# Sample tokens' layer 1 on tile B's weight chunks, an earlier sample path and new unit tables in a two-layer decoder step

## The reference

```
z = gelu(h @ w_in + b_in); u = z[:, :1536]; v = rms_norm(z[:, 1536:], g_v)     # layer 1, 1024 x 3072 weights
s = causal(w_s) . v + b_s;  y += gate * ((u * s) @ w_out)                      # 1536 x 1024
q = h @ w_q                                                                    # PEER, 1024 x 2048
idx, g = top 16 of 128 x 128 product keys, for each token and each of 8 heads
out = sum over 8 heads and 16 experts of g * gelu(u_tab[idx] . h) * v_tab[idx] # rows of 1024 floats
```

## Time and profile before

| what | value |
|---|---|
| median of three runs | 2014.44 us |
| span of the profiled execution | 2136.8 us |
| that execution against the median | 1.061 |
| TensorE, VectorE, ScalarE, GpSimd busy | 72%, 62%, 17%, 55% |
| granted TensorE clock, mean | 0.814 of full |
| moved by the DMA engines | 751.57 MB, mean 352 GB/s |
| of it by GpSimd's queue, by SyncE's queue | 564.20 MB, 185.72 MB |

### The profile page before, as it was taken

How to read it: one execution, slowest core, us unless ns; L and a number is a source line. 1 busy time by engine, 2 the same in 40 slices (tenths; PEclk the granted TensorE clock), 3 DMA queues, 4 the chain that set the end, 5 groups by cost and what they waited for, 6 DMA issues and landing times.

```text
span 2136.8 us, 25746 instructions
## 1 busy us (share of the span) xinstructions
PE 1549.0 (72%) x9280; PEld 752.4 (35%) x9280; DVE 1321.9 (62%) x3189; ACT 353.4 (17%) x934; POOL 1185.7 (55%) x1097
## 2 busy tenths in 40 slices
PE   5863767867579799878785999897877741563765
PEld 2453233522135346524442456534423310111211
DVE  2369886887776555488676756587885336434442
ACT  0210121111122111112131211131312110010011
POOL 0023665566776645467646645577675257744655
PEclk8887878987687897988887897997988785777777
DMA  9868989999999999999969799999998989999998
GB/s 371 314 236 346 365 330 347 391 396 382 347 346 348 359 404 373 361 414 347 382 212 345 271 375 401 378 345 349 367 337 303 352 309 343 402 417 370 377 349 306
DMA packets 213941, 751.57 MB, mean 352 GB/s; under 512 B 27236, under 2 KB 35628, under 8 KB 213816
## 3 DMA queue, kind: packets, MB, share of 16 engines
q0 software_dynamic: 155136, 564.20, 69.8%
q1 hardware_dynamic: 58680, 185.72, 22.4%
HBM read 747.74 MB, written 2.10 MB: 351 GB/s over the span
## 4 chain that ended last, share of the span: by engine, by line
PE 43%; DVE 14%; DMA 13%; issue 12%; POOL 8%; another core or an unknown queue 7%; ACT 2%; SPq 1%; DVEq 0%; POOLq 0%; ACTq 0%
PE yacc L1274 13%; DMA vring<-in_peer_v,expert 6%; POOL uring L813 4%; PE pp L1062 4%; DVE uring L2046 4%; POOL vring L813 3%; PE pp L1036 3%; PE pp L1125 3%; PE pq L1125 2%; PE ps L1160 2%; PE ps L870 2%; PE pp L1197 1%; DMA uring<-in_peer_u,expert 1%; PE ps L1184 1%
## 5 line engine op out<-in xcount | busy, mean ns | idle before, releaser
L813 POOL DMA_INDIRECT uring<-in_peer_u,expert x512 | 571.5, 1116 | 471.1 <-DVE dots L2046 191.1
L1274 PE MATMUL yacc<-vring,diag 64*64 64x512 f32 x4096 | 659.3, 727 | 230.1 <-DMA vring<-in_peer_v,expert 118.0
L813 POOL DMA_INDIRECT vring<-in_peer_v,expert x512 | 542.2, 1059 | 430.6 <-PE yacc L1274 263.3
L2046 DVE CUSTOM_DVE_ANT_0 uring<-uring,h 128x1024 f32<-128x1024 f32 x512 | 614.9, 1226 | 201.2 <-DMA uring<-in_peer_u,expert 175.7
L1274 PEld LDWEIGHTS yacc<-vring,diag 64*64 64x64 f32 x4096 | 158.0, 154 | 589.1 <-issue 345.5
L1566 ACT ACTIVATE diag<-cst,wts 128x64 f32<-128x64 f32 (+1 forms) x528 | 155.4, 338 | 470.4 <-PE yacc L1274 229.9
L1062 PE MATMUL pp<-hT,wring 128*128 128x128 f32 x1024 | 128.9, 287 | 10.4 <-DMA wring<-in_peer_w_q 4.6
L1062 PEld LDWEIGHTS pp<-hT,wring 128*128 128x128 f32 x1024 | 124.1, 202 | 28.1 <-issue 26.2
L1929 DVE TENSOR_REDUCE arena<-arena 128x16 f32<-128x1024 f32 x64 | 77.8, 1216 | 63.8 <-ACT arena L1505 58.8
L1317 ACT ACTIVATE arena<-ps 128x512 f32<-128x512 f32 (+6 forms) x77 | 39.9, 532 | 253.4 <-remote 76.9
L1125 PE MATMUL pp<-w_uk,arena 128*128 128x512 f32 x128 | 75.3, 677 | 3.4 <-issue 2.7
(11 more groups left out here) (306 smaller groups left out, 1823.0 us busy)
## 6 DMA issues: line engine op xcount, KB each, us to landing
wring<-in_peer_w_q SPq DMA_DIRECT2D x48, 1024.0 KB
wring<-in_sg_w_in SPq DMA_DIRECT2D x48, 768.0 KB
wring<-in_w_mod SPq DMA_DIRECT2D x35, 1024.0 KB
wring<-in_sg_w_out SPq DMA_DIRECT2D x18, 1024.0 KB
uring<-in_w_mod SPq DMA_DIRECT2D x9, 1024.0 KB, 12.7
wring<-in_mla_w_o SPq DMA_DIRECT2D x9, 1024.0 KB
uring<-in_peer_u,expert POOLq DMA_INDIRECT x512
vring<-in_peer_v,expert POOLq DMA_INDIRECT x512
```

The lines of the kernel that those rows point to most:

```text
L813: pool.indirect_dma_start(ring[:, slot % RING, :], None, table[n // 3], bass.IndirectOffsetOnAxis(ap=idx, axis=0)).then_inc(land[slot % RI ...
L1274: last = pe.matmul(yacc[64 * q:64 * q + 64, r], diag[at, slot % RING, :], v[at, 512 * q:512 * q + 512], start=first, stop=final)
L2046: dve.tensor_tensor_reduce(u, u, rows_h[:, :], 1.0, 0.0, ALU.mult, ALU.add, dots[:, p % 2, i:i + 1]).then_inc(u_used, 1)
```

## The change

- S's layer 1 input product is computed in B's `sgu_v` and `sgu_u`, with the same weight chunk in the ring; its output product in B's `sgu_out`; its layer 1 query in B's layer 1 `query` stages. The 16 `sgu_s` stages, S's own `sgu_out` and the weight part of `query_s` 5 are gone. `sgu_s_mix` stands ahead of B's `sgu_mix`.
- For that, S must be through layer 0 before B's layer 1. Caches 0 to 3 come before `peer_out` 0, caches 4 to 7 between the routes of A's layer 1, and S's experts of layer 0 after four of A's eight heads. `peer_out` 3 moves to the end.
- S's buffers su_s, sv_s, sp_s, vp_s, gT_s and the gain move into `kv` and `kr`. TensorE no longer waits for the store of new_v_s.
- The five tables are new; they hold no N.

```diff
+S_AFTER = (4, 8)
-    return a0 + b0 + a1 + b1[:2] + [(2, None)] + b1[2:8] + [(5, None)] + b1[8:]
+    return a0 + b0 + a1[:S_AFTER[0]] + [(2, None)] + a1[S_AFTER[0]:] + b1[:S_AFTER[1]] + [(5, None)] + b1[S_AFTER[1]:]
-CACHES = (2, 3, 3)
+CACHES = (4, 4)
-    era1 = ([("peer_out", 0), ("sgu_init",)] + sgu(A) +
-            heads(3, (4, 4))[:1] + mods(1, 20, 24) + woven(heads(3, (4, 4))[1:], caches[CACHE0[1]:CACHE0[2]]))
-    era2 = [("peer_out", 1)] + sgu(B) + woven(heads(4, (4, 4)), caches[CACHE0[2]:])
-    era3 = [("cache_out",), ("proj", S), ("norm", S, 0, 1), ("query_s", 2), ("topk_s", 2), ("peer_out", 3)]
-    era4 = [("peer_out", 2), ("norm", S, 1, 0)] + [("sgu_s", j) for j in range(16)]
-    era4 += [("sgu_s_mix",), ("sgu_out", S), ("norm", S, 1, 1), ("query_s", 5), ("topk_s", 5)]
-    return start + era0 + era1 + era2 + era3 + era4 + [("peer_out", 4), ("peer_out", 5)]
+    era1 = ([("peer_out", 0), ("sgu_init",), ("norm", A, 1, 0)] + sgu(A) + [("norm", A, 1, 1)] +
+            heads(3, (4, 4))[:1] + mods(1, 20, 24) + woven(heads(3, (4, 4))[1:], caches[CACHE0[1]:]))
+    era2 = [("cache_out",), ("proj", S), ("norm", S, 0, 1), ("query_s", 2), ("topk_s", 2)]
+    era3 = [("peer_out", 1), ("peer_out", 2), ("norm", S, 1, 0), ("norm", B, 1, 0)] + sgu(B)
+    era3 += [("norm", S, 1, 1), ("norm", B, 1, 1)] + heads(4, (4, 4)) + [("query_s", 5), ("topk_s", 5)]
+    return start + era0 + era1 + era2 + era3 + [("peer_out", 3), ("peer_out", 4), ("peer_out", 5)]
 PLAN_PE
-1113:VV 1114:VV 1115:VVVV 1116:VVVVVVVV
+1032:VVVVVVVVVVVVVVVVVVVVVVVVVVV 1033:VVVVV
+1039:VVVVVVVVVVVVVVVVVVVVVVVVVVVVVVVVVVVVVVVVVVVVVVVVVVVVVVVVVVVVVVVVVVVVVVVVVVVVVVVVVVVVVVVVVVVVVVVVVV 1042:VVVVVV
...
 PLAN_POOL = """
...
+UUUVUUUUUUUUUUVUVVVUVVVVVVVVVUVUVUVUUUUUUUUUUUVUVVVVVVVVVVVVVVVUUUUUUUUUUUUUUUVUVVVVVVVVUVVVVVVVUUUUUUUUUUUUUUVUVVVVV
+VVVVVVUVVVVUUUUUUUUUUUUUUVUVVVVVVVVVVVUVVVVUUUUUUUUUUUUUUVUVVVVVVVVVVVUVVVVUUUUUUUUUUUUUUVUVVVVVVVVVVVUVVVVUUUUUUUUUU
+UUVVVVVVVVVVVVVVVVV
...
+                if tile == B:
+                    last = sgu_sample(w, c, 0)
+            def sgu_sample(w, c, at):
+                last = quad_matmuls(pq[:, 1], hTs[:, c, :], w[:, 0, :], SGQ, c == 0, False)
+                if c == KD - 1:
+                    last = quad_matmuls(pq[:, 1], ones[at:at + 1, 0:32], rows[at:at + 1, :], SGQ, False, True)
+                            if lhs_s is not None:
+                                last = quad_matmuls(pq[:, 0], lhs_s[:, 32 * g:32 * g + 32], w[:, c, :], QUAD,
+                                                    g == 0, g == 2 * n - 1)
+                        if n == 4:
+                            last = quad_matmuls(pq[:, 0], hTs[:, kk, :], w[:, c, :], QUAD, kk == 0, kk == KD - 1)
-                for i in range(8):
+                for i in range(8 * (n == 2)):
-                pe.wait_ge(v_out, 80)
+                if tile == B:
+                    residual(k, S, pq[:, 0:1, :], "xs")
```

More of the change, by code:

```diff
@@ L119 @@
[L119 to L123, removed]
@@ L224 @@
 MOD_ROW = 4
-CACHES = (2, 3, 3)
-CACHE0 = [sum(CACHES[:i]) for i in range(4)]
+CACHES = (4, 4)
+CACHE0 = [sum(CACHES[:i]) for i in range(3)]
 def rope_before(b):
@@ L256, in schedule, with sgu @@
                                             ("norm", A, 0, 1)] + first[:2])
-    sgu = lambda t: ([("norm", t, 1, 0)] + [("sgu_v", t, c) for c in range(KD)] + [("sgu_vnorm", t)] +
-                     [("sgu_u", t, c) for c in range(KD)] + [("sgu_mix", t), ("sgu_out", t), ("norm", t, 1, 1)])
+    def sgu(t):
+        tail = [("sgu_s_mix",)] if t == B else []
+        return ([("sgu_v", t, c) for c in range(KD)] + [("sgu_vnorm", t)] + [("sgu_u", t, c) for c in range(KD)] + tail +
+                [("sgu_mix", t), ("sgu_out", t)])
     caches = [("cache", b) for b in range(NT)]
@@ L362, in labels @@
     if kind == "sgu_out":
-        return ["row"] * (tile != S) + [f"w{i}" for i in range(6)], ["x"], ["row"] * (tile != S)
+        return ["row"] + [f"w{i}" for i in range(6)], ["x"] + ["xs"] * (tile == B), ["row"]
     if kind == "peer_out":
@@ L374, in chunk_labels @@
     return {"mla_in": ["z", "z", "qk"], "proj": ["w0", "w1", "w2", "w3"], "query": [f"w{i}" for i in range(step[-1])],
-            "query_s": [f"w{i}" for i in range(8)], "sgu_v": ["v"], "sgu_u": ["u"], "sgu_s": ["z"],
+            "query_s": [f"w{i}" for i in range(8)], "sgu_v": ["v"], "sgu_u": ["u"],
             "sgu_out": [f"w{i}" for i in range(6)]}[step[0]]
@@ L578, in begin @@
             else:
-                if not (kind in ("sgu_v", "sgu_u", "sgu_s") and SCHEDULE[j][0] == kind):
+                if not (kind in ("sgu_v", "sgu_u") and SCHEDULE[j][0] == kind):
                     j += 1
@@ L739, in _ @@
                     sp.dma_start(su, bcast(t["sg_g_v"], P)).then_inc(gv_in, 16)
+                    for q in range(4 * (tile == B)):
+                        sp.dma_start(gv_s[32 * q:32 * q + NT, :], bcast(t["sg_g_v"][:, SGQ * q:SGQ * q + SGQ], NT))\
+                          .then_inc(gvs_in, 16)
                 spot()
@@ L1470, in query_s @@
                 after(act, PE, k, "s")
+                after(act, DVE, max(j for j in range(k) if SCHEDULE[j][0] == "route"), "top")
                 signal(copy(sc[0:64, 0, :, :], ps[1][0:64, 0:256].rearrange("p (i t) -> p i t", i=2)), "s")
@@ L1526, in sgu_v @@
                         last = copy(sv[:, 512 * q:512 * q + 512], (ps[0], ps[1], pq[:, 0])[q][:, :])
+                    if tile == B:
+                        last = copy(sv_s, pq[:, 1, 0:SGQ])
                     signal(last, "v")
@@ L1587, in _ @@
                           cache=cache, sgu_v=sgu_v, sgu_vnorm=sgu_vnorm, sgu_u=sgu_u, sgu_mix=sgu_vnorm,
-                          sgu_s=sgu_s, sgu_s_mix=sgu_s_mix, proj=projection, sgu_out=projection, peer_out=peer_out,
+                          sgu_s_mix=sgu_s_mix, proj=projection, sgu_out=projection, peer_out=peer_out,
                           tables=tables)
```

178 lines of the change are left out of this document (71 added, 107 removed), and 2 rows, old and new, of the table FLOW.

## The result

| | us, median | runs | ratio to before (95%) |
|---|---|---|---|
| kernel before | 2018.8 | 4 | 1 |
| changed kernel | 2044.9 | 4 | 1.0156 (1.0120 to 1.0192) |

The account below looks back on a forecast made before the run. It took the kernel as bound by moving its 751.57 MB, at about 85% of the best rate; terms -75 - 11 + 8 + 20 + 6 + 0 + 8 = -44 us of the 2136.8 us span gave 2093, median 1973 us, range 1900 to 2065.

Parts of the forecast that it names:

- Traffic removed, -75: Last 397 us: 27.26 MB of weight chunks fewer, at 362 GB/s, saves 75 us.
- cross-check: Whole span: 1782 us before the last stage, 271 for its 195 gathers, 12 to drain: 2065, or 2107 with losses.
- Stalls at the end, -11: End: no TensorE wait for the new_v_s store (5 us), samples' second top-16 trip covered (6): -11 (-5 to -23).
- Samples' experts of layer 0, +8 (0 to +18): Samples' top-16 and trip through memory: too few free transfers, 14 us lost less 6 for the old gap.
- B's layer 1, +20 (0 to +45): B's `peer_out` to first route's end: chain of some 225 us against 208 of transfers, 17 longer; value sums also added.
- Start +6: Start: first value sums come later, at B's first norm, most of it caught up: +6 us (0 to +17).
- caches 0: Caches 2, 3 and 5 to 7 move to other stretches, same work: 0 us (-24 to +15).
- Coarser tables, +8: GpSimd's order: 38 runs of 8 or more gathers into one ring, against 9: +8 us (-10 to +100).
- No N, 0: TensorE's table: 48 small matmuls go and nobody waits for them, no term; their effect on the clock left to a rival.
- Nothing given back: Rival, whole kernel: new order closes lulls too, traffic, end stalls and 24 us beside caches gained: 1911 us; chance 0.17.
- Clock: Rival, last 104 value sums: idle TensorE gets 1.2 GHz, sums take 1.98 us, about 35 us lost: 2006; chance 0.17.
- Runs block GpSimd: Rival, every run of 8 or more gathers: GpSimd waits on a full ring, 100 us: 2060 us; chance 0.23.

Follow-up runs that it names:

- without the trips' waits: Changed kernel with the two sample steps' gathers taking row numbers from tile B's first head, so none waits for the samples' top-16: 2033.0 us, ratio 1.0051.
- the second profile of the kernel before: The kernel before, unchanged, run and profiled once more beside the first experiments: 2012.3 us, span 2010.5 us.
- The small gathers: Both kernels with every expert's gather cut to rows of 64 floats instead of 1024: span 1926.2 us for the kernel before, 1986.8 for the changed one.
- the run with 30 fewer there: Changed kernel, end-stretch u and v gathers alternating, samples' layer-0 experts behind five steps of A's layer 1 instead of four: 2083.9 us, ratio 1.0354.
- the run with the turns: Changed kernel with u and v gathers alternating from u gather 437 on, all of the last stage: 2035.1 us, ratio 1.0074.

## Why the prediction was wrong

*What bounds the kernel: wrong, and everything else follows.* I took a DMA share of 90% and a rate of 85% of the best as a bound. With 94% of the gathers' bytes gone the kernel keeps 96% of its time. The forecast asked of each stretch how many bytes it has; it had to ask which stage chain or which issuing engine ends it.

*Traffic removed, -75: the first step that failed.* The chunks' bytes are worth 35 us, nearly all in the stretch of the samples' layer 1. By place the sum still looks near: that stretch goes altogether (-175), and the 87 gathers that it covered stand alone at the end (+107), -68 in all where I had -86 for traffic and stalls. That nearness is luck. The forecast priced neither part; it had the end stretch's length only in the cross-check.

*Where the sign turned.* The sum was -44 and the two profiled spans differ by +26: 70 us. The end and the samples' layer 1 have 18 of them, about what the runs of gathers cost. B's layer 1 has 34 (+54 for +20), the queries, routes and caches 35 (for 0), the samples' query 8 (+16 for +8). The start, A's layer 1 and the +8 for coarser tables, which has no row of its own, give 25 back. So the steps that failed most are those in which I let work moved into a stage go beside the transfers.

*The scale.* The sum was put from a span of 2136.8 on the median by 0.943. That the execution was 6% long was seen, not weighed: the rates came from it. The cross-check, 1782 us up to the last stage and 271 for it, gave 2053 before its 12 us of draining and was then scaled as well; measured are 1771 and 266. Left as it was it would have forecast no gain; and since the poor execution's rates stood in it beside the right stretches, its nearness is part luck.

*Stalls at the end, -11.* The store's 22 us stood in the stretch that went, so they are in the -175. The second trip ran covered, as forecast.

*Samples' experts of layer 0, +8 (0 to +18).* The place and the lull were right: TensorE at `peer_out`, value sums behind it, three v gathers, then the trip. The price without the trips' waits is 21 us (give or take 9), where I had 14 before taking off 6 for the old gap: within its noise of that.

*B's layer 1, +20 (0 to +45): the overlap was wrong.* The chain that I had worked out, 225 us up to the end of B's first route, came out nearly as long, in part because 9 us too much at its base met 12 too little in what came in. From the samples' `peer_out` (1394), behind which B's layer 1 begins in the changed kernel, it took 228; in the second profile of the kernel before, from B's `peer_out` (1155), 155. (From B's own `peer_out`, at 1347, it took 275, with the wait for the samples' experts in it.) The end of that route in the changed kernel:

```profile
1622.08 0.24 DVE L1844 TENSOR_SCALAR gate<-eg 128x16 f32<-128x16 f32 x1
```

But I set 208 us of transfers against it and booked little more than the 17 by which the chain was longer. The small gathers show that the transfers hold up nothing there: 168 us against 112 without their bytes. B's layer 1 alone, up to its own addition, became 168 from 114: +54. Three quarters of the products are worth 19 (I had 30 for all of them in the chain); the lull at the mixes came as forecast (160 GB/s in 1520 to 1540 us). That part of the 54 is gathers moved in (77 against 48) is not shown; the run with 30 fewer there says they cost little.

*Start +6, caches 0.* The start came 7 us earlier. For the caches: queries, routes and eight caches took 35 us more, and 52 more with the small gathers (435 + 352 + 207 against 349 + 292 + 301, cut at the same additions). So it is in the engines' own order and not in the gathers' bytes.

*Coarser tables, +8.* In the end stretch the runs cost 16 us. Ahead of it no cost of their order shows; what lumps of dots and value sums cost there is in the 35 us and was not separated.

*No N, 0: nearly right.* Their removal gained 9 us (2 to 16) in the kernel before; it was not tested in the changed one, which has none.

*The rivals.* Nothing given back: wrong, it shared the premise. Clock: wrong. TensorE was granted 0.71 in the end stretch, but a value sum took 1.25 us there (120.1 us for 768 records, 8 to a sum), not over 1.5, and the run with the turns is faster at 0.67. TensorE's group in that stretch:

```profile
L1258 PE MATMUL yacc<-vring,diag 64*64 64x512 f32 x768 | 120.1, 761 | 131.9 <-ACT diag L1551 101.0 <-DMA vring<-in_peer_v,expert 30.1
```

Runs block GpSimd: nearest in time (2060), wrong in mechanism. Its waits for rings, which answer to the last of the earlier trace rows, are 412 us, under the 454 that I gave as the mark of the forecast; but the second profile of the kernel before has 369 of them, so they did grow by 43:

```profile
POOL uring L791 <- DVE dots L2033: 212.6, 86, 11.5
POOL vring L791 <- PE yacc L1258: 199.7, 146, 18.0
```

The rate up to the last stretch was 353 GB/s (724.3 MB less 98.7, in 1771 us), over my mark of 340, and the last stretch lasted 266 us. Of the marks, the weights' bytes, both lulls and this rate came out as forecast, and the time did not: they tested the parts and not the premise. A mark for the premise would have been the rate in the samples' layer 1, 398 GB/s, against the time of that stretch with nothing but its gathers.

*What stays open.* The 35 us in queries, routes and caches (603 gathers in 1008 us, against 626 in 973). Some of it is likely the samples' last query and top-16, which moved in; no run took the top-16 out. A finer table of dots and value sums for the new order was not tried.

## What to carry to other kernels

Before pricing removed traffic by bytes over rate, ask for each stretch what would end it if its transfers were free; one run with the transfers cut small answers it for the whole kernel. A serial stage with much background work beside it is a cover: taking it out gives its length less the time that the background work takes alone, here 175 - 140 in the kernel before and 175 - 107 in the changed one. And when work moves into a stage that one engine fills already, add it to that engine's chain, whatever is transferred beside it. And of a profile 6% over the median, use the order of events and leave the rates.

## What the runs showed of the hardware

*A gather that begins while a dot runs ends some 0.8 us behind the dot.* By the timeline of the changed kernel's end stretch, the 96 gathers that overlap a dot took 1.18 us on average (17 of them over 1.5), the 87 others 0.94 (none over 1.5). In the run with the turns, where VectorE waits some 1.2 us between two dots, 170 overlap one and took 0.97 (3 over 1.5). Rows of the changed kernel's timeline, GpSimd and VectorE:

```profile
1912.21 0.93 POOL L791 DMA_INDIRECT uring<-in_peer_u,expert  x1 [0.30 <-issue]
...
1912.25 1.22 DVE L2033 CUSTOM_DVE_ANT_0 uring<-uring,h 128x1024 f32<-128x1024 f32 x1
...
1913.40 1.22 DVE L2033 CUSTOM_DVE_ANT_0 uring<-uring,h 128x1024 f32<-128x1024 f32 x1
1913.45 1.98 POOL L791 DMA_INDIRECT uring<-in_peer_u,expert  x1 [0.30 <-issue]
```

The gather that began 0.04 us ahead of a dot took 0.93 us, the one that began 0.05 us behind a dot's start 1.98. The whole trace bears the offset out: each of the 203 gathers that began 0.05 to 1.05 us behind a dot's start ended 2.02 to 2.05 us behind that start, so some 0.8 us behind the dot's own end, however early it had begun; of the 92 that had no dot at their start and a dot beginning within 0.5 us, none took over 1.17. In the run with the turns it is 170 of 170, in the second profile of the kernel before 203 of 204. The Trainium skill (GPSIMD Engine Reference, "Specifications") says that GpSimd shares its SBUF interfaces with VectorE instructions that have two SBUF inputs. The traces agree, and add the price: up to some 1.04 us for a gather that begins just behind a dot's start, next to nothing for one that begins just ahead of it. I had given that rule no chance of its own; it is worth most of the 16 us of the runs, since GpSimd's gathers in that stretch fell from 195 to 176 us busy.

*Gathers alone can hold 418 GB/s,* over 220 us, one queue, rows of 4 KB; my bound of 369 to 385 was the mean of gathers lengthened by dots. The Trainium skill (DMA: Bandwidth & Descriptors, "Where 436 GB/s comes from") takes some 358 GB/s of HBM as what binds; this run contradicts it.
